# Sums of squares of the query segments through a 128 by 16 pick matrix on TensorE, in a two-layer hybrid attention and PEER encoder

## The reference, cut to what matters

```python
def peer_ffn(h, w_q, sub_keys, u_tab, v_tab):
    ...
    def block(hb):
        q = rms_norm((hb @ w_q).reshape(PEER_BLOCK, PEER_HEADS, 2, PEER_D_KEY // 2))
        s = jnp.einsum('thpd,hpkd->thpk', q, sub_keys).astype(F32)
        v_top, i_top = lax.top_k(s, PEER_TOPK)
        ...
        u = jnp.take(u_tab, idx, axis=0)
        act = jax.nn.gelu(jnp.einsum('td,thkd->thk', hb, u).astype(F32))
        v = jnp.take(v_tab, idx, axis=0)
        return jnp.einsum('thk,thkd->td', (gate * act).astype(hb.dtype), v)
```

## Time and profile before

| | |
|---|---|
| median of 3 runs | 1622.99 us (1621.75 to 1624.92) |
| profiled execution, its own time | 1623.32 us |
| profiled execution, its span | 1621.5 us |
| mean granted TensorE clock | 0.997 of full speed |
| TensorE matmul busy | 1589.9 us, 98% of the span |
| VectorE, ScalarE, GpSimd busy | 66%, 34%, 43% |

### The profile page before, as it was taken

One profiled execution on the slowest core, in us unless ns is written; L12 is line 12 of the kernel. 1 busy time (PEld: TensorE's weight loads), 2 busy tenths in 40 slices (PEclk: granted clock), 3 DMA queues, 4 the chain that ended last, 5 costly groups with the idle time before them and its releaser, 6 DMA issues.

```text
span 1621.5 us, 31846 instructions
## 1 busy us (share of the span) xinstructions
PE 1589.9 (98%) x11548; PEld 1548.6 (96%) x11548; DVE 1065.9 (66%) x2517; ACT 544.5 (34%) x1424; POOL 698.2 (43%) x556
## 2 busy tenths in 40 slices
PE   7999999999999999999999999999999999999998
PEld 6888999999999998999978889999999999999998
DVE  4783789688886653444357847996888866544443
ACT  5675521655554000000067754226555530000000
POOL 6615614455553433343165266045535535333431
PEclk9999999999999999999999999999999999999999
DMA  9026279899999999999881252889999999999996
GB/s 359 7 100 260 92 283 338 313 409 409 409 410 387 368 409 409 410 409 410 337 290 52 98 216 92 314 332 337 410 410 409 409 360 392 410 409 410 409 410 274
DMA packets 141942, 525.77 MB, mean 324 GB/s; under 512 B 16160, under 2 KB 19744, under 8 KB 139424
## 3 DMA queue, kind: packets, MB, share of 16 engines
q1 hardware_dynamic: 86336, 322.57, 51.1%
q0 software_dynamic: 55520, 202.14, 31.8%
HBM read 523.60 MB, written 1.05 MB: 324 GB/s over the span
## 4 chain that ended last, share of the span: by engine, by line
PE 89%; DMA 4%; DVE 3%; ACT 2%; issue 1%; POOL 1%; SPq 0%; DVEq 0%; ACTq 0%; POOLq 0%
PE ps L618 87%; DMA ring<-in_peer_v 2%; PE ps L615 2%; DMA nat<-in_peer_v 1%; ACT grid L298 0%; DVE grid L1401 0%; DVE negmax L1405 0%; DMA x<-in_x 0%; DVE grid L1454 0%; ACT grid L970 0%; DVE x L1459 0%; ACT grid L1069 0%; ACT wh L1006 0%; POOL wl L587 0%; ACT grid L956 0%
## 5 line engine op out<-in xcount | busy, mean ns | idle before, releaser
L618 PE MATMUL ps<-grid,ring 128*128 128x160 f32 (+1 forms) x3712 | 523.3, 299 | 3.2 <-DMA ring<-in_peer_v 2.1
L618 PE MATMUL ps<-grid,nat 128*128 128x160 f32 (+1 forms) x3712 | 522.6, 299 | 2.1 <-DMA nat<-in_peer_v 1.2
L618 PEld LDWEIGHTS ps<-grid,ring 128*128 128x128 f32 x3712 | 508.7, 190 | 6.5 <-issue 6.3
L618 PEld LDWEIGHTS ps<-grid,nat 128*128 128x128 f32 x3712 | 508.7, 190 | 4.4 <-issue 4.4
L1683 DVE SCALAR_TENSOR_TENSOR grid<-grid,amount 128x1024 f32<-128x1024 f32 x96 | 123.3, 1285 | 151.0 <-DMA grid<-in_peer_v,lists 150.2
L600 POOL DMA_INDIRECT gath_a<-in_u_rows,lists x96 | 131.0, 1365 | 178.8 <-DVE dots L1652 124.0
L1683 DVE SCALAR_TENSOR_TENSOR grid<-gath_a,amount,grid 128x1024 f32<-128x1024 f32 x94 | 120.8, 1285 | 130.3 <-DMA gath_a<-in_peer_v,lists 128.9
L600 POOL DMA_INDIRECT gath_a<-in_peer_v,lists x96 | 112.9, 1176 | 205.6 <-PE ps L618 131.5
L580 POOL TENSOR_TENSOR wl<-grid,wh 128x512 fp32r<-128x512 f32 (+2 forms) x128 | 143.3, 1144 | 119.9 <-ACT wh L1006 98.3
L600 POOL DMA_INDIRECT grid<-in_peer_v,lists x96 | 108.4, 1129 | 175.2 <-PE ps L618 113.4
L1006 ACT ACTIVATE wh<-grid 128x512 fp32r<-128x512 f32 (+2 forms) x128 | 68.1, 575 | 321.6 <-PE ps L618 321.4
(11 more groups left out here) (198 smaller groups left out, 1767.4 us busy)
## 6 DMA issues: line engine op xcount, KB each, us to landing
nat<-in_peer_v SPq DMA_DIRECT2D x128, 512.0 KB, 13.6
ring<-in_peer_v SPq DMA_DIRECT2D x128, 512.0 KB, 13.5
nat<-in_peer_u SPq DMA_DIRECT2D x104, 512.0 KB, 7.4
ring<-in_peer_u SPq DMA_DIRECT2D x104, 512.0 KB, 7.2
grid<-in_peer_u SPq DMA_DIRECT2D x48, 512.0 KB, 6.0
grid<-in_peer_wq SPq DMA_DIRECT2D x8, 2048.0 KB, 10.0
grid<-in_w_out SPq DMA_DIRECT2D x2, 4096.0 KB, 13.3
grid<-in_w_in SPq DMA_DIRECT2D x3, 2048.0 KB, 16.6
```

The lines of the kernel that those rows point to most:

```text
L618: return nc.tensor.matmul(dst, a, b, start=first, stop=last)
```

## The change

The squares are no longer weights. A constant tile `pick` of 128 rows and 31 columns holds ones in column 15 and zeros elsewhere; its columns `15 - s` to `30 - s` are a 128 by 16 matrix whose column `s` is ones. Loaded as weights, with the 256 columns of squares passed through, it adds segment `s`'s sums to row `s` of a block of 16 rows and 256 columns in bank 0 and adds zero to the other rows. One fp32 matmul a segment (`s == 0` starts the sum, `s == 15` ends it) takes the place of the two with `ones`. [...]

After the last segment ScalarE copies the block to SBUF (`sums_sb`), and TensorE, after `early_product(0)`, waits for that copy and turns it in two transposes (16 rows by 128 columns each) into 128 rows and 32 columns, in columns 256 to 287 of bank 0. VectorE waits for those instead of for `ks_done`, and has `routing(4)` and `routing(5)` ahead of `routing(0)`.

```diff
+        pick = sb("pick", [P, 2 * NSEG - 1])
...
+        sums_sb = part(5120, SEQ)[0:NSEG, :]
...
                         for tt in range(NT):
                             tk = slice(tt * P, (tt + 1) * P)
                             mm(ps[:, 6 + s % 2, tk], qst[:, s % 2, tk], keyt[:, s, :], True, True)
-                            ins = mm(ps[:, 0, tt * NSEG + s:tt * NSEG + s + 1], qsst[:, s % 2, tk], ones[:, :], True, True)
-                        ins.then_inc(ks_done, 1)
+                        mm(ps[0:NSEG, 0, 0:SEQ], pick[:, NSEG - 1 - s:2 * NSEG - 1 - s], qsst[:, s % 2, :], s == 0, s == NSEG - 1).then_inc(ks_done, 1)
                     pe.wait_ge(pre_key[l], 16)
+                    pe.wait_ge(sel_ready, 1)
...
                         early_product(b)
+                        if b == 0:
+                            pe.wait_ge(sums_kept, past[sums_kept] + 1)
+                            for tt in range(NT):
+                                ins = nc.tensor.transpose(ps[:, 0, SEQ + tt * NSEG:SEQ + tt * NSEG + NSEG], sums_sb[:, tt * P:tt * P + P], ident[0:NSEG, 0:NSEG])
+                            ins.then_inc(sums_turned, 1)
...
                     raw_scores(NSEG - 1)
+                    A(sums_sb, ps[0:NSEG, 0, 0:SEQ], ACT.Copy).then_inc(sums_kept, 1)
...
                     if l == 0:
+                        ch.step(v.memset(pick[:, :], 0.0))
+                        v.memset(pick[:, NSEG - 1:NSEG], 1.0).then_inc(sel_ready, 1)
                         v.memset(ones[:, :], 1.0)
...
                         if n == 0:
-                            dve.wait_ge(ks_done, past[ks_done] + NSEG)
-                            ch.step(v.tensor_copy(r_ss, ps[:, 0, 0:2 * NSEG].rearrange("p (t s) -> p t s", t=NT)))
+                            dve.wait_ge(sums_turned, past[sums_turned] + 1)
+                            ch.step(v.tensor_copy(r_ss, ps[:, 0, SEQ:SEQ + 2 * NSEG].rearrange("p (t s) -> p t s", t=NT)))
...
-                    for n in (*range(20), *range(31, 39), 64, 65, *range(39, 47), 66, *range(20, 30)):
+                    for n in (4, 5, *range(4), *range(6, 20), *range(31, 39), 64, 65, *range(39, 47), 66, *range(20, 30)):
```

More of the change, by code:

```diff
@@ L318, in build @@
          lists_ready, best_shift, wexp_ready, lists_t, listt_ready, hots_ready, dist_ready, hota_act, gate_done, gated,
-         y_done, y_chunk, lam_ready, gain_in, picked, gath_used, acts_ready, yt_act, yt_dve, yt_cleared, y_turned, mean_ready, root_ready, rs0_ready, heads0_ready) = (S(n) for n in (
+         y_done, y_chunk, sel_ready, sums_kept, sums_turned, lam_ready, gain_in, picked, gath_used, acts_ready, yt_act, yt_dve, yt_cleared, y_turned, mean_ready, root_ready, rs0_ready, heads0_ready) = (S(n) for n in (
             "xsq_done xn_ready xt_done w_high w_rest w_used h_ready hsq_ready sq_used gqm_ready hn_ready rs_used kr_ready "
@@ L326, in build @@
             "lists_ready best_shift wexp_ready lists_t listt_ready hots_ready dist_ready hota_act gate_done gated "
-            "y_done y_chunk lam_ready gain_in picked gath_used acts_ready yt_act yt_dve yt_cleared y_turned mean_ready root_ready rs0_ready heads0_ready").split())
+            "y_done y_chunk sel_ready sums_kept sums_turned lam_ready gain_in picked gath_used acts_ready yt_act yt_dve yt_cleared y_turned mean_ready root_ready rs0_ready heads0_ready").split())
         PER_LAYER = {}
@@ L332, in build @@
                 (1, "rms_ready gqm_ready cqt_done cqt_ready qka_ready prepped lists_ready best_shift "
-                 "wexp_ready lists_t listt_ready acts_ready rs0_ready yt_cleared"),
+                 "wexp_ready lists_t listt_ready acts_ready rs0_ready yt_cleared sums_kept sums_turned"),
                 (2, "kr_ready up_done up_copied lam_ready y_turned mean_ready root_ready "
```

## The result

The changed kernel takes 1630.32 us (median of 6 runs, 1628.94 to 1631.63) against 1624.31 of the kernel before beside it: a ratio of 1.0043, interval 1.0033 to 1.0053. Timed once more later it took 1630.60 against 1621.13, 1.0060 (1.0047 to 1.0073). It is slower, by 6 to 9.5 us by the medians, and the two profiles differ by 7.9 us in span.

The account below looks back on a forecast made before the run. The prediction took TensorE to bound the kernel, its matmuls busy 98% of the span. From the median: 1622.99 - 0.5 (pipelined steps) + 7.8 (switches) + 0.4 (transposes) = 1630.7 us, range 1621.5 to 1640.

Parts of the forecast that it names:

- changes of shape and back: Forecast case: in TensorE's segment loop, switching between 128-column and 16-column weights makes the kernel slower, +7.8 us; chance 0.50.
- The loop has no idle time: TensorE's matmuls are busy 98% of the span, so the segment loop can't take up added switch time.
- Pipelined, the wide matmul: Key and sums matmuls of a segment, loads still going ahead: 0.89 us after 0.90, 0.22 per wide record; -0.5 us in all.
- The pair of changes: Going to 16-column weights and back around the sums matmul: 0.23 us taken, upper end 0.56.
- the uncovered 128-column load: Weight load of the group behind the sums matmul, not hidden under a running matmul: 0.10 us.
- the narrow load: Uncovered load of the 16-column sums weights: 0 to 0.10 us possible, 0.05 taken.
- an emptying: At each end of the sums matmul, overlap between following records lost in part: 0.04 us each.
- upper end of 0.56: Highest cost for going to 16-column weights and back once: 2 x 0.18 + 0.10 + 0.10 us.
- 34 pairs: Count of switches to 16-column weights and back over both layers; at 0.23 us each, +7.8 us (0 to +19).
- The covers behind the loop: After the loop, ScalarE's copy ends 1.1 us before block 0, and VectorE's sums have 2.7 us of cover: no wait.
- Pipelined changes: Rival: weight switches in TensorE's loop are pipelined or cost under 0.1 us a pair; 1622.9, up to 1626 us; chance 0.42.
- Faster by over 3.2 us: Rival for the whole kernel: its time falls by more than 3.2 us; chance 0.08.

Follow-up runs that it names:

- the 128-column run: The changed kernel with `pick` weights of 128 columns in place of 16, copy and transposes taking all 128 rows: 1621.37 us against 1623.62 of the kernel before, ratio 0.9988.

## Why the prediction came out

The forecast was 1630.7 us, slower, by changes of shape and back. The direction came out, and so did loads that don't go ahead at a change (the pick load starts with its matmul, 166.97; in the 128-column run 0.11 us before it). That the 7.7 us forecast lies between the 6.0 and 9.5 us of the two timings is partly luck: a pair was priced too low and the pairs were counted too high, and the two errors nearly cancel. Before the result the way in which a pair costs next to nothing had a chance of 0.42 against 0.50. Point by point:

- **The loop has no idle time, so its steps count one for one.** Nearly right: 30 x 0.72 = 21.6 us taken out gave 20.4 to 20.7, and the waits on V's transfers hardly moved.
- **Pipelined, the wide matmul is worth 0.01 to 0.02 us a segment.** Right in sign, slightly low: the period with 128-column weights is 3.74 to 3.75 against 3.77. The wide record was put at 0.22 us; the two cost 0.42 in the period (3.74 less the 3.32 without them), 0.21 each.
- **The pair of changes, 0.23 us taken.** That there is such a cost is shown by one column more or less (4.09 against 3.75 us); the size is 0.30. Of the parts, the uncovered 128-column load was right (0.10), and the narrow load was put at 0.05 and is 0.01 to 0.02 by the estimate above. The rest was put at 0.04 for each of the two changes and called an emptying. No row or run shows an emptying, nor the 0.18 us for it in the upper end of 0.56; in its place the runs show groups 0.10 us longer at each change (0.32 where 0.22 is undisturbed).
- **34 pairs.** Counted are the 16-column pick weights among 128-column ones, once in each of 32 segments, and the two transposes with 16 rows, once in each layer. For the transposes the runs show 0.19 us a layer (block 0 takes 2.59 us with them, 2.40 where they have 128 rows). In the loop it is one too many in each layer: segment 0's pair lies under the wait for GpSimd's weights. By these corrections the sum is 30 x 0.30 - 30 x 0.02 + 0.8 for the transposes and their changes = 9.2 us, where the chains show 8.8 and the span 7.9. No run shows the 7.8 us of the pairs; it was a term too small times a count too large.
- **The covers behind the loop.** Right, each: the copy is done 1.6 us early, the sums 2.9 us early, and with the old order there is still no visible wait.
- **The rivals.** Pipelined changes: in the 16-column kernel the loads don't go ahead, and a pair costs 0.30 us, where this rival needed less than 0.09. Faster by over 3.2 us: nothing of it is in the kernel with 128-column weights, whose ratio is 0.9988 and where the projection's 24 records still take 0.12 each (3.74 less 0.44 and 0.42 for the others).

In these traces the group ahead of a change takes 0.10 us longer, and the next weights are not loaded ahead, another 0.10 for 128 columns. What the array does at a change they can't say, since the ends of matmuls are modelled in the profile. Weights of 65 columns cost nothing against those of 128 (3.75 and 3.74 us).

## What to carry to other kernels

A matmul with few output rows is not cheap because it loads few weights: with 16 or 64 columns of weights among matmuls with 128, it paid here for going there and back, 0.3 us (periods of 4.04 and 4.09 us against 3.74), nearly as much as three weight loads of 0.11. Try such a matmul with its weights padded with zero columns (with 65 or 128 columns the cost was gone here), or gather such matmuls into one run (two in a row saved 0.28 us of the 8.09 of two segments). Before trading matmuls for fewer ones, price the records: here one with a single column passing and one with 128 cost the same 0.11 us, the time of the next load, and one with 256 cost 0.21. So one matmul with 256 columns in place of two with one column each gained next to nothing, and the 10 us came from one record in place of two, by fp32r.

## What the runs showed of the hardware that was not expected

- The price of a change of shape is about the same going in and coming out (0.10 us), and going into weights of 64 columns costs what going into 16 does (key groups of 0.54 us in both, 0.44 without a change); only what the next load then costs differs.
- Uncovered, a load of 128 columns adds 0.10 us to the period and lasts 192 ns as a record; one of 64 columns lasts 134 ns and adds 0.05 more than one of 16, which lasts 94 ns and adds an estimated 0.01 to 0.02. So the length of such a record is no measure of what the load costs; the differences between the lengths come close.
- In the profile the gap that a change leaves on the load side was put down to ScalarE's squares (0.42 us, between the pick loads and the projection's) or to "issue" (0.21 us, with two pairs a segment), neither of which held it up.
